# Constant products in TensorE's long waits, in a float32 forward pass of four blocks

## The chip, the cores and the metric

The kernel runs on one core of one Trainium2 chip. The metric is the time of one execution on the device in microseconds (us). TensorE's clock has two levels, 1.2 and 2.4 GHz; the profile gives the granted one as a share, 0.50 or 1.00.

## The reference, cut to what matters

The input is x, 512 tokens of 1024 features, float32 throughout. It passes through two models of two layers each:

```
first_block:   layer 0: x += [dilated attention, latent attention](norm(x)) @ w_out ; x += gated_ffn(norm(x))
               layer 1: x += [spatial gating, neighbourhood attention](norm(x)) @ w_out ; x += gated_ffn(norm(x))
               return norm(x)
second_block:  layer 0: x += g1 * even_mixer(modulate(norm(x)), ctx)      # gated delta rule both ways, and pooling
                        x += g2 * expert_choice_ffn(modulate(norm(x)))
               layer 1: x += g1 * short_conv_mixer(modulate(norm(x)))
                        x += g2 * expert_choice_ffn(modulate(norm(x)))
               return norm(x)

expert_choice_ffn:  aff = softmax(h @ router)                # 512 x 16
                    gate, idx = top_k(aff.T, 64)             # every expert picks 64 tokens
                    xg = h[idx]                              # gather
                    y = (silu(xg @ w_gate) * (xg @ w_up)) @ w_down * gate ; scatter-add of y to the tokens
gated delta rule:   per chunk of 64: u, wk from a triangular solve ; w = u - wk @ S ; S' = a * S + k_dec.T @ w
```

## The kernel before

Features lie on the 128 partitions and tokens along the free dimension, so x is [128, 8, 512]. The program is a sequence of blocks (`k.nc.Block`), one for the whole first model and one for each mixer and each expert layer of the second. In a block every engine has its own list of instructions, written out by hand in Python loops; semaphores (`Turns`, `Steps`) order the engines among each other, and all engines meet at the end of a block. PSUM has eight banks of 512 float32 columns; which bank a product uses is fixed by hand too.

What the change touches, in order of time:

- First block, start. TensorE sums the squares of x for the norm (`Norm.sum`, L238), computes the attention bias (L1497), then projects (`unit`, L1281) as soon as VectorE has made the tiles of h (L267). Then come the beats of the dilated attention (`first.tensor_beat`, L840 for the scores; `p` counts head pairs, `b` beats).
- First block, end. `down_stage(down1, join)` is the last down projection (L616); between its last products TensorE adds up the pairs of squares for the norm that joins the two models (`norm.sum`, L2432). The next block turns the row of sums (`turn_row`, L2445), VectorE works out the factors (L2471 to L2486), and TensorE spreads them over the partitions (`spread`, L2492).
- Even mixer. After the projections (L3351) six steps of the delta rule run, `j` from 0 to `STEPS - 1` = 5; `LAT_FROM` is 2. Of each step TensorE does: `use_state` (L2086), `keys` (L1980), `new_state` (L2096), `outputs` (L2108, L2112), then the triangular inverse by levels (`level_z` L1993, `level_update` L2007) in turn with VectorE (L2215 to L2247), then `solve` (L2064, L2071). ScalarE copies the solution out (L2172, L2174), and the next `use_state` waits for that.
- Expert layer. TensorE finishes the norm and the logits, turns x to tokens (`turn_h`, L2790) and the affinities (L2796). VectorE then picks for all experts the 64 best of 512 in `TOP` = 8 rounds of eight (`pick`, L2955, L2957, L2960). TensorE places the picks in slots (`place_slots`, L2803); GpSimd gathers the tokens by an indirect DMA (L2773); TensorE turns them (`turn_tokens`, L2816), VectorE and ScalarE copy them (L2988, L2897), and eight rounds of two experts each follow: `wide` (L2835), `down` (L2858), `combine` (L2874). The weights come through a ring of 15 slots of 1 MB. SyncE fetches a panel as soon as a slot is free. At the end `RowNorm` makes the next norm: `sums` (L2545), `turn_row` (L2556), `root`, `invert`, `spread` (L2587).
- Convolution mixer: `norm.spread`, VectorE and ScalarE make h (L2593, L2598), the units (`m.unit`, L4050), and then the block products of the output projection (`out_products`, L4055).

`k.ones` and `k.ident` are constant tiles [128, 128] that are loaded at the start and never written again.

## Time and profile before

| what | value |
|---|---|
| median of 3 runs | 2874.38 us (2871.8 to 2876.06) |
| the profiled execution's own time | 2869.82 us |
| its span | 2868.0 us |
| mean granted TensorE clock | 0.975 |
| TensorE busy | 2716.9 us, 95% |
| VectorE busy | 1132.7 us, 39% |
| weights and inputs read | 422 MB, 152 GB/s over the span |

A busy time is the share in which an engine had an instruction in work. The time in square brackets behind a row of the timeline is the idle time of that engine before it, with the engine, tile and line whose end released it. A product of float32 stands in the profile as two records, a transpose as one. Times in the rows are from the start of the span.

### The profile page before, as it was taken

The numbers are of one execution on the slowest core, as the hardware profiler recorded it, in microseconds if no ns is written. First come the engines' busy times: TensorE is split into PE (matmuls) and PEld (weight loads), VectorE is DVE, ScalarE is ACT, GpSimd is POOL, SyncE is SP. The second block draws the span as 40 slices with busy tenths as digits, with TensorE's granted clock in tenths as the row PEclk, the third lists the DMA queues.
The fourth block names the chain that finished last, engine by engine and source line by source line (L and its number), as shares of the span: only waits on it lengthen the run. The fifth ranks groups of instructions, "written<-read, shape, count | busy, mean of one in ns | idle before, by whom it ended". The sixth has DMA issues, their size and how long they took to land. (4 is left out here: it accounts for less than half of the span.)

```text
span 2868.0 us, 35950 instructions
## 1 busy us (share of the span) xinstructions
PE 2716.9 (95%) x15102; PEld 1783.4 (62%) x15102; DVE 1132.7 (39%) x2206; ACT 522.7 (18%) x1160; POOL 535.4 (19%) x371
## 2 busy tenths in 40 slices
PE   7998999999999999999999999789969999996998
PEld 4443467777886446888887745788833337872333
DVE  2315633444412233444433265655232135643223
ACT  1324421000001232101001221444011011011011
POOL 1000002333341010244442300011000004431000
PEclk9999999999999999999999999999989999998999
DMA  8110115776222221222122301100279981228994
GB/s 261 72 68 34 44 58 218 270 264 214 82 94 86 88 85 45 78 85 88 66 81 118 111 16 60 39 17 10 117 306 421 421 352 69 84 99 350 421 421 202
DMA packets 70041, 431.11 MB, mean 150 GB/s; under 512 B 8202, under 2 KB 9017, under 8 KB 25720
## 3 DMA queue, kind: packets, MB, share of 16 engines
q1 hardware_dynamic: 65080, 412.48, 37.7%
q0 software_dynamic: 4800, 16.33, 1.6%
q8 instruction: 120, 1.97, 0.3%
q14 instruction: 41, 0.34, 0.0%
HBM read 422.33 MB, written 13.79 MB: 152 GB/s over the span
## 5 line engine op out<-in xcount | busy, mean ns | idle before, releaser
L461 PE MATMUL bank<-h,weight_ring 128*128 128x256 f32 x912 | 218.8, 383 | 1.1 <-DVE arena L385 1.0
L461 PEld LDWEIGHTS bank<-h,weight_ring 128*128 128x128 f32 x912 | 170.5, 190 | 36.9 <-issue 13.3
L1281 PE MATMUL bank<-h,weight_ring 128*128 128x512 f32 (+2 forms) x464 | 183.1, 547 | 5.4 <-DVE h L267 3.4
L3351 PE MATMUL bank<-h,weight_slots 128*128 128x256 f32 (+1 forms) x576 | 174.2, 459 | 0.0
L616 PE MATMUL bank<-arena,weight_ring 128*128 128x256 f32 x704 | 155.0, 379 | 0.0
L3351 PEld LDWEIGHTS bank<-h,weight_slots 128*128 128x128 f32 x576 | 109.7, 193 | 62.6 <-issue 46.8
L2835 PE MATMUL bank<-weight_slots,tokens_T 128*64 128x512 f32 x592 | 146.2, 613 | 1.3 <-issue 1.3
L1281 PEld LDWEIGHTS bank<-h,weight_ring 128*128 128x128 f32 (+1 forms) x464 | 86.8, 193 | 96.3 <-issue 87.7
L616 PEld LDWEIGHTS bank<-arena,weight_ring 128*128 128x128 f32 x704 | 133.7, 190 | 18.6 <-issue 0.4
L461 PE MATMUL bank<-h,arena 128*128 128x256 f32 x608 | 143.6, 379 | 0.0
L461 PEld LDWEIGHTS bank<-h,arena 128*128 128x128 f32 x608 | 115.5, 190 | 15.7
L2874 PE MATMUL bank<-logits_or_select,h 128*128 128x512 f32 x256 | 118.1, 600 | 1.7 <-DVE h L3004 1.7
L616 PE MATMUL bank<-arena 128*128 128x256 f32 x528 | 117.1, 379 | 0.0
L421 POOL TENSOR_TENSOR arena<-weight_ring 128x512 f32<-128x512 f32 x38 | 48.4, 1273 | 366.5 <-PE bank L461 323.5
L319 PE MATMUL bank<-arena,weight_ring 128*128 128x256 f32 (+1 forms) x384 | 116.3, 454 | 0.0
L1281 PE MATMUL bank<-weight_ring,h 128*128 128x512 f32 x256 | 113.3, 597 | 0.0
L616 PEld LDWEIGHTS bank<-arena 128*128 128x128 f32 x528 | 100.2, 190 | 14.4 <-issue 0.9
L2835 PE MATMUL bank<-weight_ring,tokens_T 128*64 128x512 f32 x432 | 105.0, 592 | 0.0
L212 POOL TENSOR_TENSOR arena<-arena 128x512 f32<-128x512 f32 (+1 forms) x22 | 24.4, 1107 | 426.5 <-ACT arena L200 425.6
L2835 PEld LDWEIGHTS bank<-weight_slots,tokens_T 128*64 128x64 f32 x592 | 48.8, 142 | 86.0 <-issue 85.7
L763 DVE COPY arena<-bank 128x512 f32<-128x512 f32 x96 | 61.8, 685 | 91.0 <-PE bank L772 62.4
L2995 DVE TENSOR_TENSOR hidden<-bank,hidden 128x512 f32<-128x512 f32 x16 | 11.1, 692 | 216.0 <-PE bank L2835 216.0
(549 smaller groups left out, 4482.5 us busy)
## 6 DMA issues: line engine op xcount, KB each, us to landing
arena<-in_ada_w SPq DMA_DIRECT2D x48, 1024.0 KB, 5.7
weight_ring<-in_gu SPq DMA_DIRECT2D x44, 1024.0 KB, 5.0
weight_slots<-in_w_up SPq DMA_DIRECT2D x42, 1024.0 KB, 26.0
weight_slots<-in_w_down SPq DMA_DIRECT2D x34, 1024.0 KB, 21.7
weight_slots<-in_w_gate SPq DMA_DIRECT2D x32, 1024.0 KB, 22.6
weight_ring<-in_w_gate SPq DMA_DIRECT2D x32, 1024.0 KB, 23.1
weight_ring<-in_w_down SPq DMA_DIRECT2D x30, 1024.0 KB, 23.7
weight_ring<-in_down SPq DMA_DIRECT2D x32, 704.0 KB, 4.1
```

What stands on the lines that cost most here:

```text
L212: g.tensor_tensor(self.rstd[:, lo:hi], before, self.squares[:, (self.number + u) % 4, lo:hi], ALU.add).then_inc(self.folded.sem, 1)
L319: m = pe.matmul(bank, self.slots[i].buf[:, at * P:(at + 1) * P], self.src(c)[:, lo:hi], start=(c == 0), stop=(c == self.kt - 1))
L421: g.tensor_tensor(s1, self.block(q, 1, 0), self.block(q, 1, 1), ALU.add).then_inc(self.summed.sem, 1)
L461: m = pe.matmul(self.bank(q, i), weights[:, c * P:(c + 1) * P], tokens[:, c, :], start=(c == 0), stop=(c == 3))
L616: m = pe.matmul(self.bank(u, name), lhs[:, j * P:(j + 1) * P], rhs, start=(j == 0), stop=(j == self.DEPTH - 1))
L763: v.tensor_copy(self.prob_T[:, c % 2, s, :], self.k.bank[:, 4 + s, :]).then_inc(self.copied.sem, 1)
L1281: m = pe.matmul(out, lhs, rhs, start=(c == 0), stop=(c == last - 1))
L2835: m = pe.matmul(self.k.bank[e * CAP:(e + 1) * CAP, 3 + j, :], self.tok_T[:, r % 2, 4 * half + c, e * CAP:(e + 1) * CAP], slot.buf[:, c * D ...
L2874: m = pe.matmul(self.k.bank[:, 2 if n % 2 == 0 else 5, :], self.y[:, self.place(r), c * P:(c + 1) * P], self.sel[:, self.place(r), :], sta ...
L2995: v.tensor_tensor(self.hid[:, :], self.k.bank[:, 4, :], self.hid[:, :], ALU.mult).then_inc(self.product.sem, 1)
L3351: m = pe.matmul(self.bank(n)[:, 0:hi - lo], slot.buf[:, at:at + P], self.h[:, c, lo:hi], start=(c == 0), stop=(c == KT - 1))
```

## The change

A new function `stay_busy(k, pe, bank, n, cols)` issues n products of `k.ones` with `k.ident`, the latter read again for every 128 columns, into a PSUM bank; nobody reads the result, and the products signal no semaphore. It is called at these places, 512 columns wide unless HALF (256) stands there:

- first block: two after the norm's sums, one after the attention bias, two before beat 1 of the first head pair, two HALF before the join's last sums;
- even mixer: one HALF before the join's `turn_row`, four before its `spread`; in the recurrence two HALF before each `use_state` of step 1 to 5, three after the chunk ends of step 0, two (step 0) or four (steps 1 and 2) HALF after the second level, two HALF before the last `solve`, one HALF before the last `new_state`;
- each expert layer: one after each of the picks 1 to 7 (`picking`, a new wait of TensorE for VectorE's pick), nine after `place_slots`; at the end one HALF before `turn_row` and three after;
- convolution mixer: three HALF after `norm.spread`, three in the first of the output products.

```diff
--- before.py
+++ after.py
@@ -106,6 +106,12 @@
 
 
 SHARED = 8
+
+
+def stay_busy(k, pe, bank, n, cols=SEQ):
+    out = k.bank[:, bank, 0:cols].rearrange("p (n c) -> p n c", c=P)
+    for _ in range(n):
+        pe.matmul(out, k.ones, k.ident.unsqueeze(1).to_broadcast([P, cols // P, P]), start=True, stop=True)
 
 
 class Slot:
@@ -1482,6 +1488,8 @@
                     after_product = {"last": (6,), "one": (7,), "four": (8, 9)}
                     for name in d.FINAL:
                         d.product(pe, d.COUNT - 1, name)
+                        if norm is join and name == "four":
+                            stay_busy(k, pe, 5, 2, HALF)
                         for n in after_product.get(name, ()):
                             norm.sum(pe, n)
                         if name in ("three", "one"):
@@ -1491,15 +1499,19 @@
                 after(pe, const_load, 0)
                 for t in range(KT):
                     norm0.sum(pe, t)
+                stay_busy(k, pe, 0, 2)
                 pe.wait_ge(t5_in[0].sem, t5_in[0].at(0))
                 pe.wait_ge(t5_in[1].sem, t5_in[1].at(0))
                 for i in range(2):
                     m = pe.matmul(k.bank[0:HEADS, 2 + i, :], t5_sb, hot[:, i * 512:(i + 1) * 512], start=True, stop=True)
                 m.then_inc(t5_bias.sem, 1)
+                stay_busy(k, pe, 0, 1)
                 for name in proj.names[0:8]:
                     unit(pe, proj, slot, name)
                 for p in range(PAIRS + 1):
                     for b in range(BEATS):
+                        if p == 0 and b == 1:
+                            stay_busy(k, pe, 7, 2)
                         first.tensor_beat(pe, p, b)
                         if p < 4:
                             for name, i, j in fill[p].ranges(b):
@@ -2796,6 +2808,9 @@
             m = pe.transpose(self.k.bank[0:EXPERTS, 3, t * P:(t + 1) * P], self.aff[:, t, :], self.k.ident)
         m.then_inc(self.aff_T.sem, 1)
 
+    def picking(self, pe, i):
+        pe.wait_ge(self.picked.sem, self.picked.at(3 * i + 2))
+
     def place_slots(self, pe):
         pe.wait_ge(self.picked.sem, self.picked.at(3 * TOP + 9))
         for n, rows in enumerate((self.merged[0], self.merged[1])):
@@ -3084,7 +3099,11 @@
                 m.turn_affinities(pe)
                 for n in range(3, 2 * TT):
                     m.turn_h(pe, n)
+                for i in range(1, TOP):
+                    m.picking(pe, i)
+                    stay_busy(k, pe, 0, 1)
                 m.place_slots(pe)
+                stay_busy(k, pe, 0, 9)
                 m.turn_tokens(pe, 0)
                 for r in range(ROUNDS):
                     for j in range(2):
@@ -3103,7 +3122,9 @@
                     if c == KT - 2:
                         then.sums(pe, 0)
                 then.sums(pe, 1)
+                stay_busy(k, pe, 4, 1, HALF)
                 then.turn_row(pe)
+                stay_busy(k, pe, 4, 3, HALF)
                 if last:
                     then.spread(pe)
 
@@ -3705,7 +3726,9 @@
                     if n:
                         ctx_norm.ready(pe, 0, t)
 
+                stay_busy(k, pe, 5, 1, HALF)
                 norm.turn_row(pe)
+                stay_busy(k, pe, 5, 4)
                 norm.spread(pe)
                 for n in range(8):
                     conv.unit(pe, n)
@@ -3733,6 +3756,7 @@
                 c.keys(pe, 0, 0)
                 for j in range(STEPS):
                     if j:
+                        stay_busy(k, pe, 3, 2, HALF)
                         c.use_state(pe, j - 1, 0)
                         c.keys(pe, j, 1)
                         c.new_state(pe, j - 1, 0)
@@ -3748,9 +3772,12 @@
                         c.keys(pe, 0, 1)
                         gates.seen(pe, "gam_col")
                         c.chunk_ends(pe)
+                        stay_busy(k, pe, 1, 3)
                         for d in range(2):
                             c.level_z(pe, j, d, 0)
                     c.level_z(pe, j, 0, 1)
+                    if j <= LAT_FROM:
+                        stay_busy(k, pe, 3, 2 if j == 0 else 4, HALF)
                     for n in range(1, LEVELS):
                         c.level_update(pe, j, 0, n)
                         c.level_z(pe, j, 1, n)
@@ -3769,10 +3796,12 @@
                         c.keys(pe, j + 1, 0)
                     else:
                         pe.wait_ge(head.rooted.sem, head.rooted.at(MIDDLE))
+                        stay_busy(k, pe, 0, 2, HALF)
                     c.solve(pe, j)
                 for i in range(2):
                     head.spread(pe, MIDDLE, i, i)
                 c.use_state(pe, LAST, 0)
+                stay_busy(k, pe, 3, 1, HALF)
                 c.new_state(pe, LAST, 0)
                 c.outputs(pe, LAST, 0)
                 out.unit(pe, 0)
@@ -4098,6 +4127,7 @@
         self.product(pe, q, 0, self.block(q, 0, 0), self.mixes(0, 0))
         if o == 0:
             after(pe, self.quad, 7 * q - 3)
+            stay_busy(self.k, pe, 1, 3)
             pe.wait_ge(self.mixed.sem, self.mixed.at(KT - 1))
         else:
             after(pe, self.outs, 9 * (o - 1) + 5)
@@ -4276,6 +4306,7 @@
             @block.tensor
             def _(pe):
                 norm.spread(pe)
+                stay_busy(k, pe, 4, 3, HALF)
                 for i in range(2 * m.HEAD):
                     m.unit(pe, i)
                 for q in range(m.quads):
```

## Rows read from the trace of the kernel before

**Rows 1.** the page: span, engines, and PEclk, the granted TensorE clock in 40 slices.
```profile
span 2868.0 us, 35950 instructions
...
PE 2716.9 (95%) x15102; PEld 1783.4 (62%) x15102; DVE 1132.7 (39%) x2206; ACT 522.7 (18%) x1160; POOL 535.4 (19%) x371
...
PEclk9999999999999999999999999999989999998999
```

**Rows 2.** busy by stretch: length; PE, PEld, DVE, ACT, POOL; PEclk, DMA share, GB/s.
```profile
22.10:28.90 6.80, 4.21 (x10) 3.43 (x11) 6.62 (x17) 0.00 (x0) 0.58 (x1) 0.50 0.34 139
...
66.50:69.90 3.40, 3.40 (x5) 1.26 (x5) 1.21 (x4) 0.00 (x0) 0.00 (x0) 0.50 1.01 426
...
1783.40:1793.60 10.20, 6.54 (x112) 6.17 (x112) 6.46 (x19) 2.92 (x8) 0.00 (x0) 0.50 0.73 303
...
1889.20:1892.60 3.40, 3.38 (x36) 2.97 (x33) 1.90 (x4) 0.39 (x1) 1.51 (x1) 0.50 0.00 0
...
2008.70:2018.90 10.20, 9.42 (x47) 8.72 (x46) 5.82 (x13) 0.00 (x0) 0.00 (x0) 0.50 0.01 2
...
2097.40:2124.70 27.30, 8.03 (x30) 3.98 (x32) 10.55 (x42) 2.79 (x5) 3.89 (x4) 0.50 0.71 278
...
2367.10:2373.90 6.80, 5.11 (x12) 2.97 (x12) 5.01 (x8) 4.22 (x7) 6.64 (x6) 0.50 0.00 0
```

**Rows 3.** timeline, TensorE: start, length, line, shapes, count, idle before <-releaser.
```profile
1751.90 7.13 PE L3351 MATMUL bank<-h,weight_slots 128*128 128x512 f32 x16
```

**Rows 4.** timeline, TensorE, around the picks and the gather of layer 0.
```profile
2092.90 2.35 PE L2790 MATMUL bank<-constants,x 128*128 128x128 f32 x20
...
2107.07 0.60 PE L2803 MATMUL bank<-constants,merged 16*64 16x8 f32 x8 [11.82 <-DVE merged L2975]
...
2116.62 1.97 PE L2816 MATMUL bank<-constants,tokens 128*128 128x128 f32 x8 [8.95 <-DMA tokens<-tokens,slot_token]
...
2119.24 16.66 PE L2835 MATMUL bank<-weight_slots,tokens_T 128*64 128x512 f32 x64 [0.65 <-issue]
```

**Rows 5.** busy by stretch, the turning of h and the rounds of the experts.
```profile
2090.00:2096.00 6.00, 3.70 (x33) 3.17 (x31) 4.21 (x16) 4.71 (x11) 1.49 (x3) 1.00 1.04 397
...
2130.00:2340.00 210.00, 207.60 (x890) 78.30 (x886) 47.53 (x85) 19.53 (x42) 3.79 (x4) 1.00 1.01 421
```

**Rows 6.** timeline, TensorE, recurrence.
```profile
1785.62 1.97 PE L1993 MATMUL bank<-delta_masks,delta_work 64*64 64x64 f32 x32 [3.41 <-DVE delta_work L2223]
...
1790.15 1.97 PE L2007 MATMUL bank<-delta_work 64*64 64x64 f32 x32 [1.31 <-DVE delta_work L2239]
...
1826.02 1.15 PE L2007 MATMUL bank<-delta_work 64*64 64x64 f32 x32 [2.57 <-DVE delta_work L2239]
...
1861.90 1.97 PE L2007 MATMUL bank<-delta_work 64*64 64x64 f32 x32 [3.72 <-DVE delta_work L2239]
...
1882.08 2.00 PE L2064 MATMUL bank<-delta_work,weight_slots 64*128 64x64 f32 x32 [0.64 <-DVE delta_work L2247]
...
1888.14 1.09 PE L2086 MATMUL bank<-state,weight_slots 128*64 128x128 f32 x16 [2.17 <-ACT weight_slots L2174]
...
1998.41 3.68 PE L2064 MATMUL bank<-delta_work,weight_slots 64*128 64x64 f32 x32 [1.25 <-DVE delta_work L2247]
```

**Rows 7.** timeline, first attention beat, joins, out-projection of the convolution mixer.
```profile
65.15 2.01 PE L840 MATMUL bank<-arena 64*128 64x512 f32 x4 [2.69 <-DVE arena L853]
...
1561.31 1.28 ACT L2456 ACT_TABLE_LOAD   x1 [0.32 <-PEq L1332]
...
1565.97 3.78 PE L2492 MATMUL bank<-constants,join_cols 128*128 128x128 f32 x16 [4.20 <-DVE join_cols L2482]
...
2366.93 1.92 PE L2587 MATMUL bank<-constants,norm_cols 128*128 128x128 f32 x8 [1.75 <-PEq L3052]
...
2370.54 11.77 PE L4050 MATMUL bank<-h,weight_slots 128*128 128x512 f32 x23 [1.69 <-ACT h L2598]
...
2524.51 3.44 PE L4055 MATMUL bank<-mix,weight_slots 128*128 128x256 f32 x8 [3.66 <-DVE mix L4214]
```

## The prediction

> **What bounds the kernel now.** I read the page first. TensorE is busy 2716.9 of 2868.0 us and no other engine passes 1132.7, so time goes where TensorE works or waits. The clock row is at 9 in nearly every slice and falls only where the busy row falls too: a fall of the clock is the price of a wait, paid by the products behind it [rows 1]. So the second view is busy time by stretch, cut where the clock is at 0.50 (the level of 1.2 GHz; 1.00 is 2.4 GHz). The reader is to see three kinds of stretch: TensorE busy throughout and slow (66.50), mostly idle (2097.40), and one in which VectorE is busy 6.62 of 6.80 us, so that a faster TensorE gains nothing (22.10) [rows 2]. Third, the timeline shows how long each wait is that the change fills, and what the same product costs at either clock [rows 3, 4, 6, 7].
>
> **What is added.** By the diff, 47 products of 512 columns (7 and then 9 in each of the two expert layers, 15 elsewhere) and 37 of 256. A source product of float32 is two records of the profile: the 16 records of L3351 are one unit of eight products, and take 7.13 us, 0.87 us a product with the end of the last taken off [rows 3]. So a filler of 512 columns costs 0.87 us at the full clock, one of 256 columns half, 0.43, and at 1.2 GHz 1.74 and 0.87. That is 41 + 16 = 57 us of work at the full clock, on a TensorE that idles 2868.0 - 2716.9 = 151 us. Nothing is removed. The only new waits are the seven of `picking`, and they stand in a gap of TensorE's queue in which nothing but the placing of slots follows.
>
> **Does each filler fit its wait?** At the full clock:
> - Picks: the wait is 11.82 us [rows 4], a round of picks some 1.5 us (an eighth), a filler 0.87 in each of seven. The last round has none, so the placing is not held up. The following nine take 7.8 us in a wait of 8.95. Both layers alike. Fits, by 1.1 us.
> - Recurrence: three of 512 columns (2.6) in 3.41; two of 256 columns (0.87) ahead of the state's use in 2.17; four (1.74) in 2.57 and 3.72; two in 1.31; two in 1.25 ahead of the last solve [rows 6]. All fit. The one behind the last use of the state has 0.43 us and no row of its own; VectorE's operation that it lies beside is a copy-sized one. Bounds 0 and 0.43, taken 0.1.
> - Joins: the one filler ahead of the turned row at 1561 lies beside ScalarE's table load of 1.28 us; the four behind it, 3.5 us, in 4.20 [rows 7]. At the end of each expert layer one of 256 stands ahead of the turning of the row and three (1.3) behind it, where TensorE waits 1.75; three more ahead of the convolution mixer's first unit, in 1.69 [rows 7]. The first of these may hold up the row: 0 to 0.43, taken 0.1, twice. Two of 512 (1.74) before the first attention beat, in 2.69. Three (2.6) in the 3.66 of the out-projection [rows 7].
> - Start: VectorE is the bound there, so the fillers cost nothing [rows 2].
> Fillers have no reader and signal nobody, so when they fit they cost nothing. In sum 0 to 1.5 us (three times 0.43 and a little); I take 0.7, the middle.
>
> **What comes back.** Where TensorE was busy at 0.50, holding 1.00 saves half of the busy time, but only where TensorE is what the next step waits for.
> - Start, 22.10: 4.21 busy, half is 2.1; VectorE covers it [rows 2]. Take 0, bounds 0 and 2.1.
> - First beat, 66.50: 3.40/2 = 1.7 [rows 2]. The fillers end over a microsecond before the beat, so I count half: 0.85.
> - Join, 1565.97: the spread is 3.78 for 16 records [rows 7], and VectorE starts on the first eight; they go from 1.9 to 1.0. Behind it TensorE waits tile by tile for ScalarE, so the rest is covered. Take 0.9, bounds 0.5 and 1.9 (3.78/2).
> - First chunk, 1783.40: until 1790 VectorE goes from one operation to the next, so the first part gains nothing; from 1790.15 a group of 32 records costs 1.97 where it costs 1.15 at full clock [rows 6], 0.8 less, and the group behind it as much: 1.6, take 1.5 (bounds 0.8 and 6.54/2 = 3.3 [rows 2]). The same two groups at 1861.90: 1.5.
> - 1889.20: 3.38/2 = 1.7 [rows 2], less the part that waits for VectorE: 1.2.
> - Last solve, 1998.41: 3.68 against 2.00 for the same 32 records at full clock [rows 6], and as much again behind it: 3.3. Take 3.2, as the end of it lies beside ScalarE's copies.
> - 2008.70: 9.42/2 = 4.7 [rows 2], less the steps where VectorE's take and gate come between: 3.9. Only one small filler stands there, and the fillers of the last solve lie 7 us ahead. I count half: 1.95.
> - Expert layers, twice: the turning of tokens, 1.97 for eight records, goes to 1.0 (2.35 for twenty at full clock), of which 0.6 reaches the first wide product, as VectorE's and ScalarE's copies lie between. The wide products start at 2119.24 and the clock is low until 2124.7: 5.46/2 = 2.7 [rows 2, 4]. So 3.3 each, 6.6.
> - 2367.10: the spread, 1.92 to 1.0, 0.9 [rows 2, 7]; the other 3.2 of the 5.11 busy halve: 1.6. Sum 2.5. The last spread of the kernel is the same work: half of the 0.9, 0.5, as the clock falls only just before it.
> - Out-projection: 3.44 to 1.9: 1.5 [rows 7].
>
> Sum: 0.85 + 0.9 + 1.5 + 1.5 + 1.2 + 3.2 + 1.95 + 6.6 + 2.5 + 0.5 + 1.5 = 22.2 us, the full hold. From it go 0.7 for overruns and 3 us for one or two of the stretches in which the clock will still fall, since it fell after waits as short as 1.25 us (1998.41) and held through one of 2.57 (1826.02) [rows 6]: how long a wait is does not decide alone. Forecast 18.5 us. The profiled execution took 2869.8 (span 2868.0 and 1.8 around it), so it would take 2851.3; the median of the three runs is 4.6 above the profiled one, and I forecast against it: 2874.4 - 18.5 = 2855.9.
>
> **What the skill adds.** Between 2090 and 2096 TensorE did almost nothing but transposes, 3.70 us busy, and the clock read 1.00 throughout [rows 5, 4]. The Trainium skill (TensorE: Matmul & The Clock Gate, Part 4: PE-mode transpose) says that transposes do not count as busy for the clock in the way that products do. By that rule the expert layers gain less: see the third rival. The trace speaks rather against it, though it shows no long run of transposes alone.
>
> **Rivals.**
> 1. *Fillers too thin.* The clock holds where the fill is dense (picks and gather, end of a layer, 9.1 us) and falls in the recurrence and in the beats as before, perhaps elsewhere, since every later stretch is shifted. For it: falls after 1.25 and 2.17 us of wait [rows 6], where the fillers take less than half of what surrounds them. Gain 9.1 less 0.7: 8.4, time 2866.0.
> 2. *The weights set the end of the expert layers.* From 2130 to 2340 the DMA share is 1.01 at 421 GB/s while TensorE is busy 207.60 of 210 [rows 5]; both are full. If transfers are what ends the layer, the 6.6 us earned at its start become a wait for the last weights. Against it: no wait for a transfer stands in that stretch, and an earlier first round frees its slots earlier, so that transfers start again earlier too. Gain 11.9: time 2862.5.
> 3. *Transposes do not hold the clock.* Nine fillers end some 1.5 us before the tokens land; then come 1.1 us of transposes and 0.6 us of waiting. The clock falls in that gap, and the wide products begin at half clock. Loss of 2.7 in each layer: time 2861.3.
> 4. *Slower: constant products do not keep the clock up.* Then the fillers run at half clock, and the densest do not fit: nine take 15.7 in a wait of 8.95, 6.7 too long, twice; four of the join 7.0 in 4.20, 2.8; three of the first chunk and of the out-projection 5.2 each in waits of about 3.5, 3.2 together; the recurrence about 2. In all some 21 us, nothing back: 2895. It decides from the point at which the clock stays at 0.50 through the nine fillers. Against it: they are dense full-size products, and the rounds of the experts, as dense, ran at 1.00 [rows 5]. This is also the case in which the change does not do what it says.
>
> **How the numbers follow.** Forecast 0.60, rival 1 0.16, rival 2 0.11, rival 3 0.09, rival 4 0.04. The full hold with the start and the join at their upper bounds would be near 2849, the thin case 2866 with a microsecond of noise: range 2849 to 2867, with about 0.17 outside. A change of 0.2% (5.7 us, 2868.6 here) is about what a measurement of this kernel can tell. Faster takes the first four cases but for the weak tail of rivals 1 and 2: 0.89; same 0.07; slower 0.04.
>
> **What would show it.** In the changed kernel's profile: clock 1.00 through the picks, the gather and the first wide products, mean clock near 0.99; the low stretches at 1561, 2367 and 2524 gone; L2816 at about 1.1 us for its eight records, L2064 at 2.0 in the last step. Wrong would be a clock of 0.50 under fillers, a wait that has become longer than before by what precedes it (placing of slots after the last pick, L2816 later than the gather's landing), or a wait for weights in the expert rounds of some 3 us.

## The result

The changed kernel takes 2847.93 us in the median of four executions (2845.16 to 2851.47), the kernel before beside it 2873.09 (2871.69 to 2876.06): a ratio of 0.9909, interval [0.9896, 0.9922]. Three later comparisons gave 0.9915 [0.9897, 0.9933], 0.9923 [0.9907, 0.9938] and 0.9906 [0.9892, 0.9919]. The forecast was 2855.9 with a range from 2849: the direction was right, the time lies 1.1 us under the range, and the gain is some 25 us where 18.5 were forecast; the four comparisons give 25.2, 28.6, 21.8 and 24.7. Over all comparisons the 20 executions of the changed kernel have a median of 2849.5 (2845.2 to 2857.5); 55 of the kernel before, taken in four comparisons after the first, have 2874.7 (2868.0 to 2881.3).

The page of the changed kernel: its profiled execution took 2851.47 us, with a mean granted clock of 0.993 where it was 0.975. The clock row has no 8 left [rows 1], and there are 168 more TensorE records, the 84 fillers (L114). TensorE is busy 42.4 us more in a span 18.3 us shorter.

```profile
span 2849.7 us, 36285 instructions
PE 2759.3 (97%) x15270; PEld 1797.2 (63%) x15270; DVE 1134.0 (40%) x2206; ACT 522.4 (18%) x1160; POOL 536.1 (19%) x371
PEclk9999999999999999999999999999999999999999
```

Busy time by stretch of the changed kernel, layer 0 of the experts: the first seven picks, the end of the picks, the gather with the first wide products, and the rounds. It answers to the 27.30 us at 0.50 and to the rounds [rows 2, 5].

```profile
2086.00:2097.40 11.40, 7.88 (x14) 2.08 (x14) 10.55 (x41) 1.16 (x3) 1.06 (x2) 1.00 0.77 266
2097.50:2100.90 3.40, 3.20 (x11) 1.68 (x12) 0.46 (x4) 0.00 (x0) 1.80 (x2) 0.53 0.92 378
2105.00:2116.00 11.00, 9.93 (x45) 4.36 (x45) 1.37 (x4) 2.79 (x5) 0.94 (x1) 1.00 0.65 222
2116.00:2326.00 210.00, 207.60 (x893) 79.58 (x890) 45.70 (x83) 20.10 (x43) 3.79 (x4) 1.00 1.01 421
```

The timeline of TensorE in the same place (L114 is a filler, L2831 the turning of tokens, L2850 the wide product) and at the join, in the last solve and behind it. It answers to [rows 4, 6, 7]. The reader is to see that the seven picks keep their 1.49 us each, that turning takes 1.09 for 1.97 and the wide products 13.96 for 16.66, the spread of the join 2.05 for 3.78 and the solve's last step 2.00 for 3.68.

```profile
1559.43 3.70 PE L114 MATMUL bank<-constants 128*128 128x512 f32 x8
1563.12 2.05 PE L2504 MATMUL bank<-constants,join_cols 128*128 128x128 f32 x16
...
1993.77 1.13 PE L114 MATMUL bank<-constants 128*128 128x256 f32 x4
1995.10 2.00 PE L2076 MATMUL bank<-delta_work,weight_slots 64*128 64x64 f32 x32 [0.20 <-issue]
...
2086.13 1.12 PE L114 MATMUL bank<-constants 128*128 128x512 f32 x2 [0.26 <-DVE left L2975]
2087.62 1.12 PE L114 MATMUL bank<-constants 128*128 128x512 f32 x2 [0.37 <-DVE left L2975]
...
2097.70 0.60 PE L2818 MATMUL bank<-constants,merged 16*64 16x8 f32 x8 [1.50 <-DVE merged L2990]
2098.23 9.40 PE L114 MATMUL bank<-constants 128*128 128x512 f32 x18
2107.49 1.09 PE L2831 MATMUL bank<-constants,tokens 128*128 128x128 f32 x8
2109.66 13.96 PE L2850 MATMUL bank<-weight_slots,tokens_T 128*64 128x512 f32 x64 [1.07 <-issue]
```

**Where the time went, stretch by stretch.** VectorE runs the same 2206 instructions in the same order in both kernels, so the start of its n-th instruction can be compared between traces. The table is worked out that way: how many us longer a stretch took than in the first profile of the kernel before, b1 (times are those of that profile; a stretch not shown moved by under 0.3 us; the last row is the difference of the whole spans). b1 to b5 are five profiled executions of the kernel before (2869.82, 2872.79, 2871.27, 2874.30, 2869.46 us), a1 to a4 four of the changed one (2851.47, 2845.62, 2852.31, 2851.45 us).

```
stretch (what is in it)              b2    b3    b4    b5 |   a1    a2    a3    a4
   0-62   start                    -0.8  -1.0  -2.0  -0.9 | -1.7  -0.7  -0.3  -1.6
  62-80   first attention beat     -1.7  +0.8  +1.6  +1.4 | -0.8  -1.7  -1.0  -1.1
 225-250  latent attention begins  -1.0  +0.1  -1.2  +0.4 | -0.3  -1.2  -0.2  -0.3
1560-1578 join                      0.0   0.0   0.0   0.0 | -0.9  -0.9  -0.9  -0.9
1756-1779 unit rows are spread     +5.0   0.0  +5.0   0.0 | +3.4  +1.7  +3.4  +3.4
1779-1794 first chunk              +0.3   0.0  +0.2  +0.1 | -1.7  -1.7  -1.7  -1.7
1815-1824 second step               0.0   0.0   0.0   0.0 | +1.5   0.0  +1.5  +1.5
1858-1866 second chunk              0.0   0.0   0.0   0.0 | -1.5  -1.5  -1.5  -1.5
1888-1900 state use                -1.2   0.0  +0.1  +3.3 | -1.2  -1.2  -1.2  -1.2
1900-1995 solves                   +1.2   0.0  -0.1  +1.1 | -0.1  -0.1  -0.1  +0.1
1995-2024 last solve, outputs      +0.1   0.0  +0.1  -4.9 | -6.1  -7.0  -6.1  -5.9
2098-2137 picks, gather, layer 0   +0.4  +0.1  +0.3  -1.4 | -2.9  -3.3  -2.8  -3.0
2137-2345 its rounds               +0.1  +0.2  +0.1  +0.3 | +0.6  +0.5  +0.5  +0.7
2366-2387 convolution mixer         0.0  -0.1  -0.1  +1.0 | -2.4  -2.4  -2.4  -2.4
2520-2532 out-projection           -0.1  +1.6  -0.1  +0.2 | -1.5  -1.5  -1.5  -1.5
2590-2628 picks, gather, layer 1   +0.1  -0.6  +0.1  -1.4 | -2.8  -3.1  -3.1  -2.7
2628-2840 its rounds               +0.2   0.0  +0.1  +0.1 | +0.6  +0.6  +0.4  +0.6
2840-2867 last spread              +0.4  +0.4  +0.3  +0.4 | -0.5  -0.6  -0.6  -0.6
total                              +3.0  +1.5  +4.5  -0.3 |-18.3 -24.2 -17.5 -18.3
```

Two things are in it. Where the change puts fillers, nearly every row is the same in all four executions. And executions of one and the same kernel differ by whole falls of the clock (stretches in which it stands at 0.50), in a few places. One such place is new with the change: at 1815 to 1824 the clock fell in three of the four changed executions (+1.5) and in none of the five before, although TensorE's wait ahead of it is 1.10 us where it was 2.17, with two fillers in place of the rest.

### The profile page after: what moved, and what is told of

The parts are those of the page before. It is cut to its first block and busy times, and to the rows that moved or that the text cites. A ratio compares the mean times of both kernels' runs of the same rounds, so it can differ in the third digit from the quotient of the medians.

```text
span 2849.7 us, 36285 instructions
## 1 busy us (share of the span) xinstructions
PE 2759.3 (97%) x15270; PEld 1797.2 (63%) x15270; DVE 1134.0 (40%) x2206; ACT 522.4 (18%) x1160; POOL 536.1 (19%) x371
## 5 line engine op out<-in xcount | busy, mean ns | idle before, releaser
L3372 PE MATMUL bank<-h,weight_slots 128*128 128x256 f32 (+1 forms) x576 | 176.4, 462 | 0.8 <-ACT h L2517 0.8
L3372 PEld LDWEIGHTS bank<-h,weight_slots 128*128 128x128 f32 x576 | 109.5, 193 | 66.5 <-issue 49.7
L622 PEld LDWEIGHTS bank<-arena,weight_ring 128*128 128x128 f32 x704 | 133.7, 190 | 18.6 <-issue 0.4
L2850 PE MATMUL bank<-weight_slots,tokens_T 128*64 128x512 f32 x592 | 141.9, 593 | 2.1 <-issue 2.1
L467 PEld LDWEIGHTS bank<-h,arena 128*128 128x128 f32 x608 | 115.5, 190 | 15.7
L2850 PE MATMUL bank<-weight_ring,tokens_T 128*64 128x512 f32 x432 | 105.0, 592 | 0.0
L218 POOL TENSOR_TENSOR arena<-arena 128x512 f32<-128x512 f32 (+1 forms) x22 | 24.3, 1106 | 425.4 <-ACT arena L206 424.5
L2850 PEld LDWEIGHTS bank<-weight_slots,tokens_T 128*64 128x64 f32 x592 | 50.7, 137 | 80.3 <-issue 77.3
L325 PEld LDWEIGHTS bank<-arena,weight_ring 128*128 128x128 f32 x384 | 71.1, 190 | 39.1 <-issue 32.6
```

The lines of the kernel that those rows point to most:

```text
L218: g.tensor_tensor(self.rstd[:, lo:hi], before, self.squares[:, (self.number + u) % 4, lo:hi], ALU.add).then_inc(self.folded.sem, 1)
L325: m = pe.matmul(bank, self.slots[i].buf[:, at * P:(at + 1) * P], self.src(c)[:, lo:hi], start=(c == 0), stop=(c == self.kt - 1))
L467: m = pe.matmul(self.bank(q, i), weights[:, c * P:(c + 1) * P], tokens[:, c, :], start=(c == 0), stop=(c == 3))
L622: m = pe.matmul(self.bank(u, name), lhs[:, j * P:(j + 1) * P], rhs, start=(j == 0), stop=(j == self.DEPTH - 1))
L2850: m = pe.matmul(self.k.bank[e * CAP:(e + 1) * CAP, 3 + j, :], self.tok_T[:, r % 2, 4 * half + c, e * CAP:(e + 1) * CAP], slot.buf[:, c * D ...
L3372: m = pe.matmul(self.bank(n)[:, 0:hi - lo], slot.buf[:, at:at + P], self.h[:, c, lo:hi], start=(c == 0), stop=(c == KT - 1))
```

## Experiments

**One group of fillers at a time.** The first kernel keeps only the fillers of the experts' picks and gather, the second only those of the recurrence, the third all others (first block, joins, layer ends, convolution mixer); the fourth is the changed kernel, beside them. The first against the kernel before:

```diff
+                for i in range(1, TOP):
+                    m.picking(pe, i)
+                    stay_busy(k, pe, 0, 1)
                 m.place_slots(pe)
+                stay_busy(k, pe, 0, 9)
```

> Only the fillers of the two expert layers' picks and gathers (7 and 9 each). Theory of single stretches: 2.8 to 3.3 us a layer, so 5.7 to 6.6 us under the kernel before, the clock 1.00 from 2097 on and both wide stages at full clock from their first product. Rival (the fillers work together, each alone only moves the falls of the clock about): under 3 us, or a low stretch of other place that takes the gain.

> Only the fillers of the recurrence. Theory of single stretches: first chunk 1.7, chunk 2 1.5, the use of the state 1.2, the last solve 3.3, the last outputs 2 to 2.8: 9 to 10.5 us under the kernel before. Rival (the clock's falls in the recurrence are moved, not removed, as the one at 1817 of the changed kernel): 5 us or less.

> Only the fillers of the first block, the join, the layers' ends and the convolution mixer. Theory of single stretches: first beat 0 to 1.7, join 0.9, end of the first expert layer 2.4, out-projection 1.5, last spread 0.5: 5.3 to 7 us under the kernel before. With e1 and e2 the sum is then 20 to 24 us. Rival (parts do not add up): e1 + e2 + e3 differ from the changed kernel's gain in the same rounds by more than 4 us.

> The changed kernel again, unaltered, to see how far its executions spread and how its time goes with the granted clock. Theory (the time not at full clock is what the change removed, and what remains of it falls differently in each execution): median 25 us under the kernel before, executions between 2843 and 2853, those with a lower mean clock being the longer ones. Rival (one draw of the profile was lucky, the true gain is the 18.4 us that lie between the two profiled executions): median 18 to 19 us under.

Measured (interval of the ratio): e1 0.9994 [0.9985, 1.0003], 2873.05 us against 2874.76; e2 0.9963 [0.995, 0.9976], 2864.02; e3 0.9974 [0.9964, 0.9983], 2865.88; the whole 0.9915, 2846.15. The parts give 1.7 + 10.7 + 8.9 = 21.3 us, the whole 28.6. Expected were 5.7 to 6.6, 9 to 10.5 and 5.3 to 7, so the recurrence came near and the others gave more. The whole fell in two groups, four executions from 2845.2 to 2846.7 and two at 2855.1 and 2855.8, outside the 2853 expected and with the lowest granted clocks (0.991, 0.993). By means it gives 25.7 and the parts 21.4, a difference that this spread does not make sure of. The picks alone, from which 5.7 to 6.6 were expected, show no gain that can be measured. In its profile the two stretches with picks and gather are 2.8 and 1.7 us shorter, but the rounds of layer 0 give 1.2 of that back, its convolution mixer starts 0.9 worse and it had the +5.0 of 1756 to 1779. e2, which has no filler in the picks, has the gather at 0.50 for less long than b1, and gains 2.3 us in layer 0. In TensorE's timeline of e2 (L2812 the placing of slots, L2825 the turning of tokens, L2844 the wide product):

```profile
2097.33 0.60 PE L2812 MATMUL bank<-constants,merged 16*64 16x8 f32 x8 [11.83 <-DVE merged L2984]
2105.78 1.97 PE L2825 MATMUL bank<-constants,tokens 128*128 128x128 f32 x8 [7.85 <-DMA tokens<-tokens,slot_token]
2108.40 15.44 PE L2844 MATMUL bank<-weight_slots,tokens_T 128*64 128x512 f32 x64 [0.65 <-issue]
```

Here 1.1 us of the 2.3 is a transfer that landed sooner (7.85 for 8.95 [rows 4]) and 1.2 a clock that rose sooner (15.44 for 16.66). Neither is an effect of a filler in that place. Nor is it shown that fillers elsewhere did it: the kernel before has wide products of 15.3 to 15.5 us in three of the ten layers of its five profiles, one execution with +0.9 in the convolution mixer (b5) and two with the +5.0. So one profile of a part can't tell what the part is worth.

**Fillers made of transposes.**

```diff
-    for _ in range(n):
-        pe.matmul(out, k.ones, k.ident.unsqueeze(1).to_broadcast([P, cols // P, P]), start=True, stop=True)
+    for _ in range(2 * n):
+        for c in range(cols // P):
+            pe.transpose(k.bank[:, bank, c * P:(c + 1) * P], k.ones, k.ident)
```

> Every filler keeps its place and its length (eight transposes of the constant tile, 0.12 us each, for each product of 512 columns) but is made of transposes alone. Theory A (whatever keeps TensorE streaming holds the clock, transposes too): time as with products, 2846 to 2852 us, granted clock .993 or more, and 1.00 through picks and gather. Theory B (transposes do not count): the clock falls in every place in which it fell before, above all through the gather and into the first wide products of both expert layers; the fillers then run at half clock and overrun the gather as well, some 7 us in each layer, and the time is 2874 or more with a clock near .97.

Measured: 2850.29 us (2848.01 to 2853.62), ratio 0.9915 [0.9898, 0.9931]. Theory A holds. A window and the timeline of its gather in layer 0 (the column after POOL's is the clock), then the timeline of layer 1:

```profile
2097.30:2107.70 10.40, 8.77 (x83) 8.51 (x84) 0.84 (x6) 0.00 (x0) 2.95 (x3) 1.00 0.99 404
```

```profile
2098.29 8.08 PE L114 MATMUL bank<-constants 128*128 128x128 f32 x72
2107.34 1.09 PE L2831 MATMUL bank<-constants,tokens 128*128 128x128 f32 x8 [0.98 <-DMA tokens<-tokens,slot_token]
...
2593.67 1.09 PE L2831 MATMUL bank<-constants,tokens 128*128 128x128 f32 x8 [2.57 <-DMA tokens<-tokens,slot_token]
2595.84 15.65 PE L2850 MATMUL bank<-weight_slots,tokens_T 128*64 128x512 f32 x64 [1.07 <-issue]
```

In layer 0 the clock is 1.00 through 72 transposes, the wait behind them and the 8 that turn tokens. The Trainium skill (TensorE: Matmul & The Clock Gate, Part 4: PE-mode transpose) says that the full clock does not engage for transposes, as they do not count as busy in the same way. The trace does not agree: fillers of transposes held the clock as those of products do, with one exception in this profile. In layer 1 the tokens landed later, TensorE waited 2.57 us, and the clock fell for 3.4 us at the start of the wide products (15.65 where the changed kernel has 13.95). e1, whose fillers are products, has such a fall in the same place (15.55), so it does not speak against transposes. By the rule this kernel would have taken 2874 us or more, Theory B.

**Fillers of 8 rows.**

```diff
-        pe.matmul(out, k.ones, k.ident.unsqueeze(1).to_broadcast([P, cols // P, P]), start=True, stop=True)
+        pe.matmul(out, k.ones[0:8, :], k.ident[0:8, :].unsqueeze(1).to_broadcast([8, cols // P, P]), start=True, stop=True)
```

> Every filler keeps its place, its count and its columns, but its two tiles have 8 rows in place of 128, as the products that spread a unit row have, in whose run at 1759 to 1773 us the clock falls although TensorE is busy. Theory A (how full TensorE's rows are matters for the clock, not only whether it is busy): the clock falls in the picks, the gather and the recurrence nearly as before; fillers at half clock overrun the gather by up to 6.7 us in each layer; time 2870 to 2890, clock .97 to .98. Theory B (being busy is enough, and the fall at 1759 has another cause, such as the short waits between the products): time 2846 to 2852 at .993 or more.

Measured: 2892.16 us (2889.85 to 2895.42), ratio 1.0067 [1.005, 1.0083], clock 0.972. Theory A, and more than it said. The timeline of picks and gather:

```profile
2097.72 1.12 PE L114 MATMUL bank<-constants 8*128 8x512 f32 x2 [0.26 <-DVE left L2975]
2099.21 10.39 PE L114 MATMUL bank<-constants 8*128 8x512 f32 x12 [0.37 <-DVE left L2975]
2109.53 0.60 PE L2818 MATMUL bank<-constants,merged 16*64 16x8 f32 x8
2110.06 15.72 PE L114 MATMUL bank<-constants 8*128 8x512 f32 x18
2125.71 1.97 PE L2831 MATMUL bank<-constants,tokens 128*128 128x128 f32 x8
```

The first filler still took its 1.12 us at the full clock; then it fell, six fillers took 10.39 and fill the picks to the last, and nine took 15.72, 6.8 us more than the wait of 8.95 that they stand in [rows 4]. With the same number of columns in the same places, a TensorE busy at 8 of its 128 rows did not keep its clock. The time is 2.2 us above the 2870 to 2890 that were expected. This is the slower rival's mechanism, priced there at 15.7 for the nine and 2895 for the kernel, with another cause: not constant data but thin products.

**Twice the fillers in the gather.**

```diff
-                stay_busy(k, pe, 0, 9)
+                stay_busy(k, pe, 0, 18)
```

> Eighteen products instead of nine after the slots are placed, in both expert layers. 18 x 0.87 = 15.7 us in a wait of 8.95. Theory A (a filler costs what it overruns, at its full length): 6.7 us later in each layer, 13.5 us in all over the changed kernel, 2860 to 2862. Theory B (the weights set the pace of the last rounds, so that a late start is partly made up, as an early one was partly given back): under 12 us over the changed kernel, because the last rounds, which now take 0.6 us more than 29.08 each layer, fall back to 29.08.

Measured: 2864.62 us (2860.04 to 2866.72), ratio 0.9966 [0.9953, 0.9978].

```profile
2097.18 15.72 PE L114 MATMUL bank<-constants 128*128 128x512 f32 x36
2112.74 1.04 PE L2831 MATMUL bank<-constants,tokens 128*128 128x128 f32 x8
```

The stretches of picks and gather are 6.4 and 6.3 us longer than in a2: what overruns costs its full length, Theory A. The rounds did not make any of it up (+0.5 in each layer, as in a2). Between the medians are 15 us where 13.5 were expected; of what the two layers leave, 2.8 is in this profile for a fall between 1952 and 1959 us.

**The kernel before, again.** Four more profiled executions.

> The kernel before, once more, for a second profiled execution of it. Theory A (the stretches in which the clock falls differ from one execution to the next of the same kernel): the stretch from 1756 to 1779 us differs from the first profile's by up to 5 us, and the execution is nearer to 2874 than to 2869.8 us. Theory B (they are a property of the kernel's order of work): every low stretch stands where it stood, and every stage is within 0.3 us of the first profile.

> The kernel before, a third profiled execution. Theory A (its executions differ by which of a few stretches lose the clock, and the first profile was a cheap draw): against the first profile 0 to 5 us more from 1756 to 1779 us, 0 to 1.3 from 1900 to 1995, the other stretches within 0.5 but the first beat (0 to -1.7) and the start of the latent attention (0 to -1.2); execution of 2870 to 2878 us, in which these differences add up to the difference in time. Theory B (something spread over the whole span, such as the transfers, makes them differ): the differences do not add up in these stretches.

> As the third profile; a fourth draw. By theory A at least one of the two is above 2873 us and has the falls of 1756 to 1779 at 3.3 to 5 us.

> As the third profile; a fifth draw. Mean of the five executions by theory A 2872 to 2875 us.

The results are b2 to b5 of the table: Theory A. The differences lie in whole falls in few places: 5.0 in two of five at 1756, 3.3 and -4.9 at 1888 and 1995 in b5, up to 3.3 between executions in the first beat; the 1310 us from 250 to 1560 agree within 0.03. Busy time from 1756 to 1779 in b3 and then in b4, TensorE never idle in either, clock 0.93 and 0.70:

```profile
1756.00:1779.00 23.00, 23.00 (x70) 11.27 (x70) 9.01 (x15) 1.05 (x2) 0.00 (x0) 0.93 0.00 1
```

```profile
1756.00:1779.00 23.00, 23.00 (x46) 10.92 (x45) 8.74 (x14) 1.05 (x2) 0.00 (x0) 0.70 0.00 1
```

So no execution was free of it: the clock falls once there in b1, b3 and b5, twice and for longer in b2 and b4. The mean of the five is 2871.5 us, half a microsecond under what was expected, and 3.2 under the median of the 55 others.

**What loses the clock at 1756 to 1779.** TensorE's timeline of b1 there, and then of a1 (L3441 and L3462 spread the unit rows, 8 rows of TensorE each; L3351 and L3372 are the convolution's units). No row has a wait before it, and still 16 records of 256 columns take 5.41 us:

```profile
1758.97 3.69 PE L3441 MATMUL bank<-gate_rows,delta_masks 8*128 8x512 f32 x8
1762.59 5.41 PE L3351 MATMUL bank<-h,weight_slots 128*128 128x256 f32 x16
```

```profile
1755.21 3.69 PE L3462 MATMUL bank<-gate_rows,delta_masks 8*128 8x512 f32 x8
1758.83 5.41 PE L3372 MATMUL bank<-h,weight_slots 128*128 128x256 f32 x16
1764.17 4.84 PE L3462 MATMUL bank<-gate_rows,delta_masks 8*128 8x512 f32 x8
1768.94 9.34 PE L3372 MATMUL bank<-h,weight_slots 128*128 128x512 f32 x16
```

First the thin products were interleaved with the units instead of standing four in a row:

```diff
             m = pe.matmul(...)
+            if between:
+                if c == KT - 1:
+                    m.then_inc(self.done.sem, 1)
+                between(c)
...
+                    conv.unit(pe, n, (lambda c, n=n: units.spread(pe, 4 * (n - 33) + c // 2) if c % 2 else None) if n >= 33 else None)
```

> The changed kernel, with the products that spread the unit rows (8 rows of TensorE each) issued one behind every second product of the convolution units instead of four in a row. No wait is filled or opened by it. Theory A (a run of products of 8 rows loses the clock although TensorE is busy): the falls between 1757 and 1773 us go, the stretch from 1756 to 1779 takes at least 3.3 us less than in the first profile of the changed kernel and is the same in every execution; the median falls by 2 to 5 us, to 2842 to 2845, and the executions lie closer together. Theory B (the clock falls there for the short waits around the solve's start, not for the thin products): the falls stay, time within 1 us of the changed kernel's.

> The changed kernel, unaltered, beside the two above on the same chip. 2846 to 2851 us, with granted clocks from .991 to .996 and the time falling as the clock rises.

Measured: 2852.40 us (2849.22 to 2856.0) against 2851.82 for the changed kernel beside it (2847.82 to 2857.53): no gain. The fall of 1757 was gone, but another came, and it is among the thin products again. From its timeline (L3467 is the spread):

```profile
1763.20 1.12 PE L3467 MATMUL bank<-gate_rows,delta_masks 8*128 8x512 f32 x2
1764.25 1.70 PE L3372 MATMUL bank<-h,weight_slots 128*128 128x256 f32 x4
1765.88 2.07 PE L3467 MATMUL bank<-gate_rows,delta_masks 8*128 8x512 f32 x2
1767.88 3.77 PE L3372 MATMUL bank<-h,weight_slots 128*128 128x512 f32 x4
```

Beside the units of 256 columns the thin products take as much of TensorE's time, 1.12 beside 1.13 us, as the full ones. So this did not tell the theories apart. And the order has a price of its own. In the profile of the next kernel with this order (e8, below) the clock stays at 1.00 through all thin products, and a unit of 256 columns with its four thin products takes 8.45 us (1760.46 to 1768.91). Apart, at the same clock, they take 7.1: 3.45 for the unit (e9, 1758.89 to 1762.34) and 3.63 for the four (b1, 1767.93 to 1771.56). For the three units that is some 4 us, which hides what a saved fall gives. The first chunk behind lost the clock too (+0.8 instead of -1.7). The next kernel changes the rows alone; the rows beyond the eight are zeros of the table of constants:

```diff
+        units.tall = rows[:, 0:1024].rearrange("p (s t) -> p s t", s=2)
...
-        pe.matmul(self.k.bank[:, 2 + m % 4, 0:tok], self.dm["row_pick"][0:8, i * P:(i + 1) * P], self.norm_rows[:, p, 0:tok],
+        pe.matmul(self.k.bank[:, 2 + m % 4, 0:tok], self.dm["row_pick"][:, i * P:(i + 1) * P], self.tall[:, p, 0:tok],
```

> The changed kernel, with the twelve products that spread the unit rows given all 128 rows of TensorE (the rows beyond the eight are zeros of the constant table) in place of 8. Order, count, columns and waits stay, and so does what is computed. Theory A (the clock falls between 1757 and 1775 us because those products use 8 rows): the low stretches there go, the stretch from 1756 to 1779 is 3.3 us shorter than in the profiles of the changed kernel that have two low stretches, and the conv units behind it run at 1.00; median 2 to 4 us below the changed kernel's beside it. Theory B (the half-wide products of the context units, or something outside TensorE, lose the clock): the falls stay where they are, time within 1 us of the changed kernel's.

> The changed kernel, unaltered, beside the two above on the same chip: 2846 to 2851 us.

Measured: 2845.14 us (2843.45 to 2848.15) against 2851.30 (2846.56 to 2852.61) beside it, ratios 0.989 [0.9875, 0.9906] and 0.9906. The same four rows of its timeline:

```profile
1755.46 3.60 PE L3462 MATMUL bank<-gate_rows,delta_masks 128*128 128x512 f32 x8
1758.89 3.62 PE L3372 MATMUL bank<-h,weight_slots 128*128 128x256 f32 x16
1762.34 3.60 PE L3462 MATMUL bank<-gate_rows,delta_masks 128*128 128x512 f32 x8
1765.78 7.03 PE L3372 MATMUL bank<-h,weight_slots 128*128 128x512 f32 x16
```

Four such products cost nearly the same with 8 rows or 128 (3.69, 3.60), and the units behind take 3.62 and 7.03 instead of 5.41 and 9.34. The stretch is 5.8 us shorter than in a1 and 2.5 shorter than in b1, which had lost the clock there once as well. Theory A, by more than the 2 to 4 us that were expected. A fall of 3.4 us came instead at 1776.64, over the chunk ends, products of 8 rows again (row_pick, L1982); it cost 0.7 us of the first chunk's gain.

**The two waits left empty.** Fillers for the waits of 2.61 and 3.97 us in which the latent attention begins. This one (e8) stands on the interleaved kernel, e7, and ran beside it.

```diff
+                        if p == 4 and b in (4, 5):
+                            stay_busy(k, pe, 2, 2 if b == 4 else 3)
                         first.tensor_beat(pe, p, b)
```

> The kernel above, with two and three more fillers of 512 columns in the two waits at the start of the latent attention (2.61 and 3.86 us long, at about 229 and 237 us), which the change leaves empty. Theory A (what the clock gives back there is as everywhere: half of TensorE's busy time behind the wait where TensorE sets the pace): 0.9 to 1.3 us less than the kernel above, the low stretches between 227 and 241 us gone. Theory B (VectorE and ScalarE set the pace there, as in the start-up): no gain, and up to 0.5 us for what overruns.

I had counted the beats wrongly: these fillers went one head pair late, where TensorE had 0.36 us of wait. Measured: 2855.10 us (2853.92 to 2865.55), slower than both kernels beside it (2852.40 and 2851.82). In its timeline they stand at full price, 1.88 and 2.74 us, and the stretch is 3.6 us longer:

```profile
259.11 1.88 PE L114 MATMUL bank<-constants 128*128 128x512 f32 x4
...
263.41 2.74 PE L114 MATMUL bank<-constants 128*128 128x512 f32 x6
```

With the fillers in pair 3, between the score and the turn of beat 4 and ahead of beat 5, on top of e9:

```diff
+                        if p == 3 and b == 4:
+                            first.score(pe, p, 3)
+                            stay_busy(k, pe, 6, 2)
+                            first.turn(pe, p - 1, 1)
+                        else:
+                            if p == 3 and b == 5:
+                                stay_busy(k, pe, 6, 3)
+                            first.tensor_beat(pe, p, b)
```

> The kernel above, with two and three fillers of 512 columns in the two waits of 2.61 and 3.97 us at 228 and 237 us. The earlier attempt at this put them one beat late, at 259 and 263 us, where TensorE did not wait, and they cost 3.6 us at their full length. Theory A: as everywhere, what comes back is what the products behind the wait lose at 0.50 where TensorE sets the pace: the stretch from 225 to 250 us is 0.9 to 1.2 us shorter and no low stretch is left in it. Theory B (VectorE sets the pace there): no gain within 0.2 us.

Measured: 2844.00 us (2843.64 to 2844.36), ratio 0.9884 [0.9869, 0.99], against 2845.14 for e9. The stretch from 225 to 250 is 1.3 us shorter than in e9 and 2.1 than in a1, and the clock does not fall in it; Theory A. The medians alone, 1.1 us apart with executions of e9 on both sides, would not tell. The timeline, with the waits now 0.69 and 2.80:

```profile
226.40 1.98 PE L114 MATMUL bank<-constants 128*128 128x512 f32 x4
229.08 1.25 PE L760 MATMUL bank<-constants,arena 128*128 128x128 f32 x8 [0.69 <-DVE arena L769]
230.17 1.88 PE L1287 MATMUL bank<-weight_ring,arena 128*128 128x512 f32 x4
231.89 2.74 PE L114 MATMUL bank<-constants 128*128 128x512 f32 x6
237.43 1.25 PE L760 MATMUL bank<-constants,arena 128*128 128x128 f32 x8 [2.80 <-DVE arena L769]
```

This version beats both kernels, by 7 us the changed one beside it, and its four executions lie within 0.7 us where those of the changed kernel spread over 6 to 11 in a comparison.

## Why the prediction was right or wrong

**The steps that held.** The profiled execution was forecast at 2851.3 us and took 2851.47. Of the terms of the sum, forecast and a1 to a4: join 0.9, 0.91; first chunk 1.5, 1.7; second chunk 1.5, 1.5; state use 1.2, 1.2; convolution mixer 2.5, 2.4; out-projection 1.5, 1.5; last spread 0.5, 0.55; expert layers 6.6, 5.7 to 6.4 (but see the second rival). So half of TensorE's busy time at 0.50, where TensorE is what the next step waits for, is what holding the clock gave back. Fillers that fit cost nothing: TensorE picks up its work in the seven picks as it did. The start was rightly put at 0: its 0.3 to 1.7 us are no more than b2 to b5 show without fillers. The agreement of 2851.3 with 2851.47 is in part luck: a2, the same kernel, took 2845.62.

**The terms that were off.** Last solve and outputs were 3.2 + 1.95 = 5.15 and measured 5.9 to 7.0. The halving of the outputs was wrong: the clock stayed up through most of them, and in a2 through all (the forecast's own full value, 3.2 + 3.9 = 7.1). The half for the first beat, 0.85, was reached (0.8 to 1.7), but the kernel before differs there by 3.3 us between its own executions. Overruns were near 0 and not 0.7, but for some 0.2 us where nine fillers at partly 0.53 took 9.40 us.

**The step that failed** is the last of the sum. The prediction took off "3 us for one or two of the stretches in which the clock will still fall", and then set the remaining 18.5 against the median, because it stood 4.6 us above the profiled execution. The 18.5 is a difference of two single executions, b1 and one of the changed kernel. Carried over to the medians, it holds only if the changed kernel's median stands 4.6 above its profiled execution too. It stood 3.5 below it in the first comparison (2847.93 against 2851.47), and 2.0 below over all 20. These two, 4.6 and 3.5, less the 0.2 by which the profiled execution was missed, are the whole miss of 8.0 us. b1 was a cheap draw: other executions of the kernel before have falls that it lacks (5.0 us more at 1756 in two of five, 3.3 at 1888 in b5, 1.2 and 1.1 at 1900 in b2 and b5).

The deduction itself was right in kind: a1 has +3.4 at 1756 and +1.5 at 1815. But the kernel before pays at 1756 too, 2.0 us more than b1 in the mean of its five profiles against 2.9 in the mean of the four of the changed one. So only 0.9 there and 1.1 at 1815, some 2.1 of the 3 us, is a loss by the change. Mean against mean (2871.5 and 2850.2) the gain is 21.3 us: 24.3 in the places where less time is lost, less those 2.1 and 0.9 in the rounds. That 22.2 - 0.7 = 21.5 comes so near is again luck.

**What the prediction held of the clock** was too narrow: "a fall of the clock is the price of a wait". At 1762.9 it falls in b1 with TensorE busy throughout; e5 and e9 show that products of 8 rows do it. The prediction names no place of this kind.

**What stays open.** Medians differ by 25.2 us, 3.9 more than those means, mostly because the five profiled executions of before lie 3.2 under the median of the 55 others. The granted clock, on record for every execution, accounts for a part: 30 of the 55 ran at 0.974 or less, one of the five did, and the median is 2875.9 at 0.974 (25 executions) and 2872.6 at 0.975 (20). But at the same rounded clock the profiled ones are still 1.6 to 1.8 us faster. Where the others lost it, and what the rest is, isn't known. Nor is why the clock fell at 1815 only with the change.

**The rivals.** 1 (fillers too thin) is refuted: one of 0.87 us in each 1.49 held the clock through seven picks at 1.00, though in a1 it fell for 3.4 us behind them; what it feared for the recurrence came in two places, at 1815 and, for 3.4 us, at 2002, each in three of four. 2 (the weights set the end of the layer) is true for a sixth of its price. The first round went from 19.2 to 16.05 us, and the last two of seven from 29.08 and 29.40 to 29.27 and 29.82: 0.6 us in each layer is given back, not 3.3. In both kernels no wait for a transfer is recorded there, and DMA moves 421 GB/s throughout; what takes the 0.6 was not tried apart. So the expert layers gave 4.4 to 5.3 and not 6.6. 3 (transposes do not hold the clock, and the wide products begin at 0.50) is refuted by the changed kernel itself, whose wide products take 13.95 or 13.96 us in all eight layers profiled, and its reason by e4; in e1 and e4 the clock did fall there, once each. 4 is refuted for products of 128 rows, and its price came true, 2892 for 2895, for those of 8.

## What to carry to other kernels

Judge a stretch for the clock by what TensorE's rows show and not by its busy time alone: short waits and runs of thin products both cost it, and both could be mended here at no cost, by products that nobody reads in a wait that they fit, and by zero rows in a product that is thin. Price a filler at nothing only if the wait holds it in the worst execution; what overruns, or stands where TensorE doesn't wait, costs its full length. And where executions differ by discrete events, take several profiles of the kernel before and compare means with means: a gain read from one execution does not carry over to a median, and a deduction for events that both kernels suffer belongs on both sides.

## What the runs showed of the hardware

- The order of products has a price: four products of 8 rows put one by one between the products of a unit of 256 columns took 8.45 us with it, and 7.1 apart from it, both at 1.00.
- Products of 8 rows take about as long as those of 128 (3.69 and 3.60 us for eight records of 512 columns) and do not keep the clock up: the same fillers gave 2849 us with 128 rows and 2892 with 8.
- Fillers of transposes alone kept it at 1.00 for 8.08 us, and the kernel's time within a microsecond of that with products (2850.3 and 2849.5). Once, behind a wait of 2.57 us, it fell at the start of the wide products, as it did once with products (e1).
- No effect of the content showed: constant tiles, all but one in 128 of the moving one zero, and zero rows below eight that count, held it as the kernel's own data do.
- Whether the clock falls in a given place differs between executions of one kernel, by up to 5.0 us in a stretch with no wait at all, while 1310 us of it repeat within 0.03. With few falls left the spread went from 13 us (2868.0 to 2881.3, 55 executions) to under 1 (2843.6 to 2844.4, but only four).
